# Six banks for x's first transposes, K's products ordered by operand, and loads and remainders moved at the two seams of a hybrid block

## The reference

```python
h = rms_norm(x, ln_g)
proj = einsum('bsd,de->bse', h, w_in)          # 1024 x 2560
u_pool, g_pool, c_a, c_b, g_conv, q, k, v, g_attn = split_columns(proj)
y_pool = pool_mixer(u_pool, pool_w, pool_scale)         # trailing means over 2, 4, 8, 16 tokens, linear map, scale
y_conv = conv_module(c_a, c_b, dw, dw_b, ln_g, ln_b, pw)  # GLU, causal conv of 31 taps, LayerNorm, silu, 256 x 256
y_attn = sliding_window_attention(q, k, v, sinks)       # 8 query, 2 key heads, window 128, ALiBi, sinks
y = concat([y_pool * silu(g_pool), y_conv * silu(g_conv), y_attn * silu(g_attn)])
out = rms_norm(x + einsum('bse,ed->bsd', y, w_out), final_g)
```

## Time and profile before

| | |
|---|---|
| runs (us) | 1419.88, 1416.33, 1419.55 |
| median | 1419.55 us |
| the profiled execution | 1420.05 us, its span 1418.3 us |
| granted TensorE clock, mean | 0.998 |
| TensorE busy | 1392.4 us (98%) |
| VectorE, ScalarE, GpSimd busy | 1188.9, 553.0, 384.5 us (84%, 39%, 27%) |
| DMA | 196.91 MB, mean 139 GB/s |

### The profile page before, as it was taken

One profiled execution on the slowest core, in us unless ns is written; L12 is line 12 of the kernel. 1 busy time (PEld: TensorE's weight loads), 2 busy tenths in 40 slices (PEclk: granted clock), 3 DMA queues, 4 the chain that ended last, 5 costly groups with the idle time before them and its releaser, 6 DMA issues.

```text
span 1418.3 us, 20098 instructions
## 1 busy us (share of the span) xinstructions
PE 1392.4 (98%) x6814; PEld 1138.8 (80%) x6814; DVE 1188.9 (84%) x2455; ACT 553.0 (39%) x1428; POOL 384.5 (27%) x592
## 2 busy tenths in 40 slices
PE   6999999999999999999999999999999999999997
PEld 4878787787878787878888888888888888888886
DVE  5787878787878776677999998989999998898886
ACT  5666565555565554422122112121132243333332
POOL 5122323324232333120001011010110355555551
PEclk9999999999999999999999999999999999999999
DMA  9616071525343324535123033030327575555531
GB/s 214 202 29 252 17 241 62 200 104 171 125 163 133 134 119 117 210 61 206 35 114 134 15 149 133 15 133 34 145 97 275 237 241 175 179 175 162 163 108 75
DMA packets 89366, 196.91 MB, mean 139 GB/s; under 512 B 13904, under 2 KB 55248, under 8 KB 81616
## 3 DMA queue, kind: packets, MB, share of 16 engines
q1 hardware_dynamic: 65616, 172.48, 34.2%
q10 hardware_dynamic: 23680, 23.60, 6.4%
HBM read 114.27 MB, written 81.79 MB: 138 GB/s over the span
## 4 chain that ended last, share of the span: by engine, by line
PE 83%; DVE 12%; SPq 1%; ACT 1%; DMA 1%; issue 1%; ACTq 0%; POOLq 0%; POOL 0%; DVEq 0%
PE wide L345 11%; PE wide L347 11%; PE wide L346 11%; PE pair L1145 10%; PE pair L1149 10%; PE pair L1146 9%; DVE m_tail L1896 5%; PE pair L1127 3%; PE wide L1163 2%; PE wide L1164 2%; PE turn L347 2%; PE turn L345 2%; PE turn L346 2%; PE pair L347 2%; PE pair L345 2%; PE pair L346 2%
## 5 line engine op out<-in xcount | busy, mean ns | idle before, releaser
L1896 DVE SCALAR_TENSOR_TENSOR m_tail<-m_tail,m_taps 128x512 f32<-128x512 f32 x480 | 338.4, 750 | 4.6
L1145 PE MATMUL pair<-xT,w_hi 128*128 128x512 f32 x632 | 252.9, 400 | 6.3 <-DVE w_lo L409 4.6
L1149 PE MATMUL pair<-xT,w_hi 128*128 128x512 f32 x632 | 248.1, 393 | 0.0
L1146 PE MATMUL pair<-xT,w_lo 128*128 128x512 f32 x632 | 247.6, 392 | 0.0
L107 POOL TENSOR_TENSOR pool_carrier<-pool_carrier 128x1 f32<-128x1 f32 x77 | 27.0, 351 | 707.4 <-DVE m_meanvar L1905 400.1
L1649 POOL TENSOR_TENSOR operand_sums<-m_y 128x512 f32<-128x512 f32 x75 | 102.1, 1362 | 167.7 <-PE wide L347 116.6
L1145 PEld LDWEIGHTS pair<-xT,w_hi 128*128 128x128 f32 x632 | 119.3, 189 | 33.7 <-DVE w_lo L409 5.0
L1149 PEld LDWEIGHTS pair<-xT,w_hi 128*128 128x128 f32 x632 | 119.0, 188 | 29.5 <-DVE xT L338 2.6
L1146 PEld LDWEIGHTS pair<-xT,w_lo 128*128 128x128 f32 x632 | 119.4, 189 | 21.7
L774 POOL TENSOR_SCALAR a_rows<-a_rows,a_inv 128x128 f32<-128x128 f32 x256 | 109.1, 446 | 76.5 <-DVE a_inv L974 76.5
L345 PE MATMUL wide<-x_first,w_hi 128*128 128x512 f32 x320 | 125.5, 392 | 0.0
(11 more groups left out here) (261 smaller groups left out, 2925.7 us busy)
## 6 DMA issues: line engine op xcount, KB each, us to landing
xT_scratch<-xT SPq DMA_DIRECT2D x16, 2048.0 KB, 8.5
x_first<-xT_scratch SPq DMA_DIRECT2D x16, 1024.0 KB, 7.9
xT<-xT_scratch SPq DMA_DIRECT2D x16, 1024.0 KB, 9.1
combo_scratch<-stage SPq DMA_DIRECT2D x28, 512.0 KB, 4.1
m_y<-y_scratch ACTq DMA_DIRECT2D x14, 1024.0 KB, 6.7
xs<-in_x_dram SPq DMA_DIRECT2D x20, 512.0 KB, 8.7
y_scratch<-y_out SPq DMA_DIRECT2D x8, 1024.0 KB, 4.2
y_scratch<-y_out SPq DMA_DIRECT2D x16, 512.0 KB, 2.8
```

The costliest lines, as they stand in the source:

```text
L1145: nc.tensor.matmul(out, w_hi, st.hi[:, kk, :], start=(kk == 0), stop=False)
L1146: nc.tensor.matmul(out, w_lo, st.hi[:, kk, :], start=False, stop=False)
L1149: last = nc.tensor.matmul(out, w_hi, st.lo[:, kk, :], start=False, stop=(kk == KT - 1))
L1896: nc.vector.scalar_tensor_tensor(out=conv[:, i, :], in0=h[:, i, j:j + TB], scalar=taps[:, i, j:j + 1], in1=conv[:, i, :], op0=ALU.mult, op ...
```

## The change

The first six pieces of x are transposed before K, in six banks (`TURNS = 6`, with q1's bank `proj[1]` as the sixth). K's projection of block 0 is written out in `first_keys`: the high products of the six pieces, the low-weight products of the six, the transposes of the last two, the low-x products of the six, then the last two triples. K's two parts on ScalarE are issued one square earlier. GpSimd makes the bias only after x's last low part. In the last attention block the weight loads on ScalarE stand behind k's rounding, and GP's low weights behind sub-block 3. The five pool loads go from SP to ScalarE, and VectorE prepares the pool ahead of the taps.

```diff
-TURNS = 4
+TURNS = 6
@@ attention_programs
-    st.use(turn + [score[:, 2 * b:2 * b + 2].rearrange("p a b -> p (a b)") for b in (2, 3)],
+    st.use(turn + [score[:, 2 * b:2 * b + 2].rearrange("p a b -> p (a b)") for b in (1, 2, 3)] + [proj[1][:]],
@@ gpsimd
+        pool.wait_ge(st.lo_done, KT)
         alibi(1, 1)
         alibi(0, 4)
@@ scalar
         st.load_gain(act)
-        st.first_square(act, range(0, 3))
+        st.first_square(act, range(0, 2))
         w.load(act, CHUNK_K, (2, 3))
-        st.first_square(act, range(3, SUB))
+        st.first_square(act, range(2, SUB))
         w.load(act, CHUNK_Q, (2, 3))
@@ scalar, body
                 st.split_hi(act, n, kk)
-                if first and kk == 3:
+                if first and kk == TURNS - 1:
                     w.split_hi(act, CHUNK_Q, 0)
...
                 if not final:
                     st.load(act, n + 1, (2, 3))
-                else:
-                    act.wait_ge(st.lo_done, KT * NB)
-                    for c in (CHUNK_CB, CHUNK_CA, CHUNK_GP):
-                        w.load(act, c, (2, 3))
             act.wait_ge(proj_full, filled(n, slot("k")))
...
             last.then_inc(k_hi_done, 1)
+            if final:
+                act.wait_ge(st.lo_done, KT * NB)
+                for c in (CHUNK_CB, CHUNK_CA, CHUNK_GP):
+                    w.load(act, c, (2, 3))
             q_hi(n, 0)
@@ vector, body
-                if final and j == 2:
+                if final and j == SUB - 1:
                     w.split_lo(dve, CHUNK_GP)
@@ tensor
+        def first_keys():
+            c, out, cols = CHUNK_K, proj[0][:], slice(0, P)
+
+            def product(kk, w_part, x_part):
+                return nc.tensor.matmul(out, w_part(c)[:, kk, cols], x_part[:, kk, :],
+                                        start=(kk == 0 and w_part == w.hi and x_part is st.hi),
+                                        stop=(kk == KT - 1 and x_part is st.lo))
+
+            turned, rest = range(TURNS), range(TURNS, KT)
+            pe.wait_ge(w.hi_done, w.hi_count(c, 0))
+            for kk in turned:
+                pe.wait_ge(st.hi_done, kk + 1)
+                product(kk, w.hi, st.hi)
+            pe.wait_ge(w.lo_done[c], 1)
+            for kk in turned:
+                product(kk, w.lo, st.hi)
+            for kk in rest:
+                st.transpose(pe, kk)
+            for kk in turned:
+                pe.wait_ge(st.lo_done, kk + 1)
+                product(kk, w.hi, st.lo)
+            for kk in rest:
+                pe.wait_ge(st.hi_done, kk + 1)
+                product(kk, w.hi, st.hi)
+                product(kk, w.lo, st.hi)
+                pe.wait_ge(st.lo_done, kk + 1)
+                last = product(kk, w.hi, st.lo)
+            last.then_inc(proj_full, 1)
...
                 st.first_transposes(pe)
-                project(n, "k", lambda kk: st.transpose(pe, kk + TURNS) if kk + TURNS < KT else None)
+                first_keys()
                 project(n, "q0")
@@ mixer_output_programs, sync
         sp.dma_start(pw[:], conv_pw[0].rearrange("(i p) d -> p i d", p=P)).then_inc(small_loaded, 16)
-        sp.dma_start(pscale.rearrange("p i d -> p (i d)"), pool_scale[0:1, :].to_broadcast([P, 2 * P])).then_inc(pool_w_loaded, 16)
         w.load(sp, CHUNK_GC)
-        sp.wait_ge(pool_w_zero, 1)
-        for g in range(4):
-            half = slice(g % 2 * 64, g % 2 * 64 + 64)
-            sp.dma_start(pool_map[half, g // 2, half], pool_w[0, g]).then_inc(pool_w_loaded, 16)
@@ scalar
+        def load_pool():
+            act.wait_ge(score_full, ATTENDED)
+            act.wait_ge(score_taken, ATTENDED)
+            act.dma_start(pscale.rearrange("p i d -> p (i d)"), pool_scale[0:1, :].to_broadcast([P, 2 * P])).then_inc(pool_w_loaded, 16)
+            act.wait_ge(pool_w_zero, 1)
+            for g in range(4):
+                half = slice(g % 2 * 64, g % 2 * 64 + 64)
+                act.dma_start(pool_map[half, g // 2, half], pool_w[0, g]).then_inc(pool_w_loaded, 16)
...
+        load_pool()
         blocks(act, mixer_body)
@@ vector, mixer_body
                 dve.wait_ge(halo_zero, 2)
+                prepare_pool()
                 prepare_taps()
                 some_taps(m, r, 0, 2)
-                prepare_pool()
                 turn_u()
```

## The result

The changed kernel is slower, not faster: 1424.16 us median (1422.57 to 1424.74) against 1419.41 (1416.33 to 1421.63) in the same comparison. The ratio is 1.0027, its 95% interval 1.002 to 1.0035, where 0.9974 was forecast. The profiled execution took 1423.83 us, with a span of 1422.1 against 1418.3.

The account below looks back on a forecast made before the run. TensorE bounds the kernel, busy 1392.4 of 1418.3 us, leaving 26 us idle plus slow-paced work. Terms 1.7 - 0.2 + 0.2 + 0.7 + 1.2 + 0.2 = 3.8 us, from the median 1419.55 to 1415.8 us; range 1413.3 to 1418.0.

Parts of the forecast that it names:

- part 4: Last attention block: weight loads behind k's rounding win 0.2 us; GP's later low weights end the 0.7 wait on a_pT.
- Part 1: Start: K's weights asked for sooner land at 14.6 us, 0.3 us of gain, bounds 14.0 to 15.9.
- Rival B: Start: Q's parts share the transfer with K's last ones, K lands at 15.9, 1416.9 us; chance 0.10.
- Part 2: Start: six banks and K's products by operand; first product at 16.2, q0 at 26.8 against 28.48, 1.7 us won.
- Part 3: Start: GpSimd's later bias is hidden but meets VectorE's w_lo under an exclusive lock; 0.2 us lost at q2, bound 1.1.
- Part 5: Near the end: pool's loads on ScalarE's queue win 1.2 us on m_sums and 0.2 on m_tail.
- rival E: Near the end: pool_map lands late on ScalarE's queue; slower from a landing at 646.1, 1421.5 us at 648; chance 0.04.
- GP's own 0.7: Last attention block: moving GP's low weights later removes TensorE's wait of 0.7 us on a_pT.
- Slower: Whole kernel: the outcome that the change makes it slower, given a chance of 0.04.

Follow-up runs that it names:

- e2: The kernel before with one edit: GP's low weights made behind sub-block 3 instead of 2; ratio to before 1.0025.
- e4: The kernel before with only the six banks, K's products by operand and the later bias, K asked for as before; ratio 0.9992.
- e6: The kernel before with only K's two parts on ScalarE issued behind the square of row 1; ratio 0.9999.
- e8: The kernel before with only the end changes (weight loads behind k's rounding, pool's loads on ScalarE, pool prepared first), without GP's move; ratio 0.9978.
- e9_gp_after_second: The changed kernel with GP's low weights made behind the second scores of sub-block 3; ratio to before 0.9999.
- e1: The changed kernel with GP's low weights made behind sub-block 2 again; ratio to before 0.9969, median 1416.45 us.
- e3_gp_between: The changed kernel with GP's low weights made between the first and second scores of sub-block 3; ratio to before 0.996, median 1414.88 us.
- e3_again: The same kernel as e3_gp_between, timed in another comparison; ratio to before 0.9972, median 1415.86 us.
- e5: As e3_gp_between, but ScalarE issues its two of K's parts behind the square of row 2, as before the change; ratio to before 0.9965.
- e7: As e3_gp_between, but GpSimd makes the bias directly behind the reciprocal roots again; ratio to before 0.9968.
- e11: The kernel before with the end changes and GP's low weights between the scores of sub-block 3, start unchanged; ratio 0.9976, median 1417.65 us.

## Why the prediction was wrong

**The step that failed is one clause of part 4**: "GP's low part is not wanted before gp0, some 30 us on; behind it stand y_out's copy and pT". It named two kinds of followers: the product that reads the result, and what is queued behind on VectorE. There is a third, who waits for the operand to be read: SyncE, which overwrites `spare`. Its wait stood in the profile of before, 32.4 us long, and SyncE's waits were not read, since a queue that waits looks like a cost to nobody. That the slack was too small could have been had from that profile. w_lo from behind sub-block 2 to behind sub-block 3: its end from 617.1 to about 624; landing 4.7 behind the issue at 617.11; wanted 12 products into cb0, at 626.4. That is a slack of 4.6 against a move of 7, a stand of 2.4. It came out at 5.3, because the rest of the change took from the slack as well: the load moved by 7.5 and took 0.4 longer, and TensorE reached cb0 2.0 sooner (621.57 against 623.58), which makes 7.5 + 0.4 + 2.0 - 4.6 = 5.3.

**The clock added to it.** Each of the four stands, 3.1 to 5.2 us long, was followed by slow products (0.43 instead of 0.23): for 3.2 us after the one of 3.1, 3.4 after 4.1, 2.7 after 5.2 (e2) and 4.6 after 5.2 (the changed kernel), 1.5 to 2.3 us on top. The length of the stand does not order them. Waits of 1.4 and 2.2 us on m_sums (e4, e6) had no slow products behind them. The Trainium skill (TensorE: Matmul & The Clock Gate, Part 1) lets the rate follow how busy the engine has recently been; the windows above agree, 1.00 before the stand, 0.81 over it and 0.50 after it.

**Step by step, the rest:**

- Part 1, K sooner: forecast 0.3 won, found nothing. K's landing goes with that of x's last row, which varies by 3.4 us over the 14 profiles. "x and K together take the same time, whoever asks first" was borne out and should have made the term zero. Rival B (K at 15.9) is not needed for 15.59: the five other profiles with K asked for as before all lie above 14.89 themselves.
- Part 2, banks and order: from K's landing to q0 the forecast has 12.2 us against 13.59 before, 1.4 won. The nine profiles with the new order have 10.8 to 12.0, mean 11.4; the five with the old order 11.4 to 13.6, mean 12.8: 1.4 won in the means, though the two ranges overlap (e2 has 11.4 with the old order). So this term is borne out by the profiles; the timed 1.1 us of e4 does not contradict it. The first product at 17.36, outside the forecast's 16.2 +- 0.5, was off by K's late landing (15.59 against 14.6), and the six low products, amid which the pace rose, took 1.8 to 2.8 us. q0 at 27.37 is inside the forecast's bounds; it waited 0.2 us for Q's low weights, where the forecast had the two paths meet.
- Part 3, bias: the mechanism was right, its place small. In the profile of before K's w_lo took 2.15; started first, it takes 1.2, and it is GpSimd's affine_select that takes twice as long. From e2 and e8:

```profile
16.25 1.22 DVE L409 TENSOR_TENSOR w_lo<-a_rows,w_hi 128x1024 fp32r<-128x1024 f32 x1 [3.49 <-ACT w_hi L404]
16.27 2.16 POOL L746 TENSOR_SCALAR_AFFINE_SELECT a_gate<-a_gate 128x1024 f32<-128x1024 f32 x1
```

```profile
16.14 1.09 POOL L746 TENSOR_SCALAR_AFFINE_SELECT a_gate<-a_gate 128x1024 f32<-128x1024 f32 x1
16.14 2.16 DVE L409 TENSOR_TENSOR w_lo<-a_rows,w_hi 128x1024 fp32r<-128x1024 f32 x1 [3.51 <-ACT w_hi L404]
```

  In the earlier trace rows, too, the affine_select began 20 ns ahead and kept its 1.09. It is whichever comes second, by as little as that, which waits out the other. That is the exclusive lock which the Trainium skill (SBUF — State Buffer, "SBUF: two separate sides") describes, and not a sharing. The 0.2 forecast as lost at q2 was not: the second w_lo of Q took 2.29, and q2 kept its distance from q0, 11.26 us against 11.27.
- Part 4, k: a_k_lo gone, q1 at 560.91 with the 0.23 on a_q that was forecast; that is 1.28 sooner than before, 1.11 of it the start, so 0.17 against the forecast's 0.2. Right. a_pT gone: right.
- Part 5: m_sums and m_tail gone, pool_map in time (no rival E). In the profiles 1.35 and 0.5 against 1.2 and 0.2; timed, part 5 with k brought 3.1 (2.0 to 4.4) against 1.6. The one profile that the forecast read had the shortest of the three waits on m_sums. That this explains all of the difference is not shown. Of the 0.5 behind map_u 0.2 is m_tail; the rest was not traced.
- The sum: 3.8 forecast for all, of which GP's own 0.7. Without GP's move 3.1 forecast, 4.4 (2.8 to 5.8) measured. One smaller slip: rival B's 1.3 us on 1415.8 is 1417.1, not 1416.9.

The rivals were all about the start, pool's loads, or waits of TensorE that replace one another; none was about memory that a moved instruction frees. Slower was given 0.04, and to the wrong mechanism.

## What to carry to other kernels

When an instruction is moved later, list three followers: who reads its result, who is queued behind it on its engine, and who waits to overwrite what it reads. The third is found in the waits of the DMA queues and in the addresses of the buffers, not in TensorE's list. And a loss that lands ahead of an existing wait may look smaller alone (4.2 us behind q0 here) and cost more in a kernel from which that wait has been removed (6.9).

## What the runs showed of the hardware

- Six executions with one and the same start had x's last row in SBUF anywhere from 8.5 to 11.2 us. A gain of 1 us there can't be read from two profiles. The stretch from K's landing to q0 is steadier: 10.8 to 12.0 us in the nine profiles with the new order.
- TensorE's pace rose from 0.43 to 0.23 us a product 3.5 us after K's first product in one execution (17.53 to 21.0, e2) and 5.9 us after it in another of the same order (18.18 to 24.1, before), with TensorE busy throughout. q0 came 9.05 us after K's first product in the one and 10.30 in the other. What makes the difference was not found. That this is the clock is read from the pace there: the granted clock reads 1.00 over the slow stretch of before as well. In e9_gp_after_second the granted clock itself shows it (the second window holds K's slow products, which began at 15.65 after 2.6 us of waiting; busy TensorE and instructions, granted clock, DMA share, GB/s):

```profile
12.00:15.00 3.00, 0.93 (x7) 1.00 1.14 191
15.50:21.50 6.00, 5.84 (x12) 0.50 1.13 196
22.50:25.00 2.50, 2.50 (x15) 1.00 1.13 200
```

- The four equal issues of pool_map took a median of 7.9 us to land on ScalarE's queue in the changed kernel, and 5.8 on SyncE's in the one before. It is not the queue: in the seven profiles with the issues on ScalarE and `x_first`'s quarter loaded in time (e1, e3_gp_between, e3_again, e5, e7, e8, e11) the median was 4.1 to 4.7. In the changed kernel the issues, from 627.7 on, fell into the quarter's own late load. It made no difference there, since VectorE asked for pool_map only at 644.1, some 6 us behind the landing.
